# Cache copies issued earlier on the scalar engine, and the end of the second last expert in another order

## What is computed

```python
q, k, v, u = rms(x) @ w_in                       # 12 heads of 64, and 1280 pool channels
x = x + concat(dilated_attention(q, k, v), pool(u) @ pool_w * scale) @ w_out
mk, mv = rms(mem) @ w_ck, rms(mem) @ w_cv        # 256 memory rows of the prompt
x = x + cross_attention(rms(x) @ w_cq, mk, mv) @ w_co
e, gate = route(rms(x))                          # the best 2 experts of one group of 8, 4 groups
x = x + sum(gate * (silu(h @ w_gate[e]) * (h @ w_up[e])) @ w_down[e])
win_k_sample = concat(cache_win_k[:, 1:], k_new) # 8 sequences x 2048 rows x 768 numbers, values alike
```

## Time and profile before

| | us |
|---|---|
| runs shown | 1520.78, 1521.37, 1527.52 |
| median | 1521.37 |
| the profiled execution's own time | 1515.31 |
| its span (first to last instruction) | 1513.5 |
| PE busy | 1271.1 (84%) |
| DVE busy | 531.9 (35%) |
| ACT busy | 167.1 (11%) |
| mean granted clock of PE | 0.885 |

### The profile page before, as it was taken

The page is one execution under the profiler, slowest core; times in us unless marked ns, Lnnn a source line. Parts: engine busy times, 40 slices in busy tenths (PEclk is TensorE's granted clock), DMA queues, the critical chain, the costliest instruction groups (busy, mean ns, idle before and its releaser), DMA issues.

```text
span 1513.5 us, 31182 instructions
## 1 busy us (share of the span) xinstructions
PE 1271.1 (84%) x14012; PEld 741.9 (49%) x14012; DVE 531.9 (35%) x1105; ACT 167.1 (11%) x395; POOL 65.3 (4%) x118
## 2 busy tenths in 40 slices
PE   7999999998999999877778777777777877777776
PEld 4444468765887776443443343334344334333432
DVE  2220155740113326344234334334323433433433
ACT  3100113320111334000000000000000000000000
POOL 2100022221100000000000000000000000000000
PEclk9999999999999999888888788788788878878878
DMA  9999989999999999999999999999999999999997
GB/s 351 347 389 388 352 313 392 381 331 377 389 398 384 367 390 384 385 429 430 435 434 433 430 430 430 435 433 432 432 430 430 433 433 433 433 430 430 433 430 294
DMA packets 87644, 609.43 MB, mean 403 GB/s; under 512 B 6095, under 2 KB 7818, under 8 KB 72722
## 3 DMA queue, kind: packets, MB, share of 16 engines
q1 hardware_dynamic: 44867, 477.13, 75.2%
q10 hardware_dynamic: 34550, 100.80, 18.1%
q0 software_dynamic: 8176, 30.78, 5.8%
HBM read 603.09 MB, written 106.75 MB: 469 GB/s over the span
## 4 chain that ended last, share of the span: by engine, by line
DMA 56%; PE 41%; DVE 2%; issue 1%; ACT 0%; SPq 0%; DVEq 0%; ACTq 0%
DMA ring<-in_w_e_up_dram 46%; PE pb L1152 11%; PE pb L660 7%; PE pb L906 6%; DMA ring<-in_w_in_dram 5%; DMA ring<-in_w_out_dram 5%; PE pb L742 3%; PE pb L1039 2%; PE pb L924 2%; PE pb L686 1%; DMA ring<-in_w_ck_dram 1%; PE pb L710 1%; PE pb L666 1%; PE pb L1186 1%; PE pb L1092 1%
## 5 line engine op out<-in xcount | busy, mean ns | idle before, releaser
L1152 PE MATMUL pb<-ring,xT 128*32 128x128 f32 x8192 | 279.9, 303 | 108.0 <-DMA ring<-in_w_e_up_dram 103.2
L1152 PEld LDWEIGHTS pb<-ring,xT 128*32 128x32 f32 x8192 | 259.0, 123 | 162.8 <-DMA ring<-in_w_e_up_dram 127.4
L2035 DVE TENSOR_TENSOR Z<-pb,Z 128x512 f32<-128x512 f32 x248 | 152.7, 679 | 267.8 <-PE pb L1109 267.8
L1092 PE MATMUL pb<-Z,xT 128*32 128x512 f32 (+1 forms) x768 | 133.9, 789 | 93.5 <-DVE Z L2035 91.5
L1109 PE MATMUL pb<-xT 32*128 32x512 f32 x744 | 172.7, 756 | 0.7 <-DVE Z L2035 0.7
L1186 PE MATMUL pb<-ring,xT 128*32 128x512 f32 x960 | 153.7, 798 | 3.4 <-issue 3.4
L660 PE MATMUL pb<-ring,hreg 128*128 128x512 f32 (+1 forms) x320 | 125.7, 552 | 2.4 <-DMA ring<-in_w_in_dram 2.4
L1092 PEld LDWEIGHTS pb<-Z,xT 128*32 128x32 f32 (+1 forms) x768 | 16.4, 115 | 181.5 <-DVE Z L2035 118.8
L660 PEld LDWEIGHTS pb<-ring,hreg 128*128 128x128 f32 x320 | 60.1, 190 | 64.9 <-issue 59.2
L906 PE MATMUL pb<-hreg,ring 128*128 128x264 f32 x320 | 77.7, 400 | 5.4 <-DMA ring<-in_w_out_dram 5.4
L1186 PEld LDWEIGHTS pb<-ring,xT 128*32 128x32 f32 x960 | 34.8, 141 | 95.6 <-issue 94.9
(11 more groups left out here) (338 smaller groups left out, 1099.3 us busy)
## 6 DMA issues: line engine op xcount, KB each, us to landing
ring<-in_w_e_gate_dram SPq DMA_DIRECT2D x31, 4096.0 KB, 23.2
ring<-in_w_e_down_dram SPq DMA_DIRECT2D x30, 4096.0 KB, 17.6
ring<-in_w_e_up_dram SPq DMA_DIRECT2D x30, 4096.0 KB, 23.7
out_win_k_sample_dram<-in_cache_win_k_dram ACTq DMA_DIRECT2D x24, 1536.0 KB, 15.7
out_win_v_sample_dram<-in_cache_win_v_dram ACTq DMA_DIRECT2D x24, 1536.0 KB, 16.9
ring<-in_w_in_dram SPq DMA_DIRECT2D x7, 4096.0 KB, 33.5
ring<-in_w_out_dram SPq DMA_DIRECT2D x4, 4096.0 KB, 34.7
out_win_k_sample_dram<-in_cache_win_k_dram ACTq DMA_DIRECT2D x8, 1488.0 KB, 15.8
```

The lines of the kernel that those rows point to most:

```text
L1092: last = mm(pb[0][32 * c:32 * c + 32, :], pick[0:n, t, :], xn[0:n, t, 512 * c:512 * c + 512], start=(t == 0), stop=(t == 2))
L1152: last = mm(pb[1][32 * c:32 * c + 32, P * half:P * half + P], XT[:, k, :], w[:, k, P * c:P * c + P], start=(k == 0), stop=(k == KT - 1))
L2035: last = V.tensor_tensor(d, banks[c][:, :], d, ALU.add)
```

## The change

Two edits.

1. The copies that ACT issued in the loop over the pool map (behind tiles 6 and 9) are gone there, and its loop over the turned token tiles issues six instead of four. The count runs on, so the same quarters go out in the same order, and between the two places every call issues a quarter that comes two later.
2. In the second last expert PE runs the sample tokens' `combine` ahead of `gather`, into a bank of its own (`pb[2]`, which else holds the turned gates), `gather` doesn't wait for DVE there, and the gates are turned behind `down`. DVE reads that bank, and its loop ends one expert earlier, with the second last written out.

```diff
                 for t in range(3):
-                    if t == 1 and not (isinstance(i, int) and i < 2):
+                    if t == 1 and not (isinstance(i, int) and (i < 2 or i == NE - 1)):
                         pe.wait_ge(y_added, 3 * i - 4)
...
+                if last_but_one:
+                    combine(i, 2, pb[2:3])
+                    gather(i + 1)
+                    return
                 if not last_of_all:
                     gather(i + 1)
...
+            def down_and_gates():
+
+                pe.wait_ge(hidT_ready, NE - 1)
+                down(NE - 2)
+                pe.wait_ge(y_added, 3 * (NE - 2))
+                turn_gates(NE - 2)
+
             with pe.If(n_over > 0):
-                down(NE - 2)
+                down_and_gates()
...
             with pe.Else():
-                down(NE - 2)
+                down_and_gates()
...
             for k in range(KT):
                 freed(copy(xT[:, k, :], filled("x")[:, 0:TOK]))
-                if k % 4 == 3:
+                if k in (1, 3, 5, 7, 11, 15):
                     cache_part()
...
                 freed(nc.scalar.mul(mixP[:, j, :], filled("map")[:, 0:TOK], gT[:, 4 * KT + j:4 * KT + j + 1]))
-                if j in (6, 9):
-                    cache_part()
...
-                    add_results(i, 2, pb[0:1] if last_of_all else pb[4:8])
+                    last_but_one = isinstance(i, int) and i == NE - 2
+                    add_results(i, 2, pb[0:1] if last_of_all else pb[2:3] if last_but_one else pb[4:8])
...
-            with dve.Fori(1, NE - 1) as i:
+            with dve.Fori(1, NE - 2) as i:
                 expert(i)
+            expert(NE - 2)
```

## The result

The changed kernel takes 1524.47 us, median of 20 runs (1519.33 to 1537.9); the kernel before, in the same session on the same chip, 1520.57, median of 20. The ratio is 1.0037, 95% interval 1.0020 to 1.0054: 5.6 us slower (3.0 to 8.2). The ratio and its interval come from all the runs; the two medians alone lie 3.9 us apart. The time lies within the range and within the 0.5% that the prediction called no change, but on the other side: it had forecast 2.4 us faster.

What follows compares the result with a forecast made beforehand. The prediction took weight transfers to set the pace from 643 us on, with PE busy nearly throughout before 590. Its terms, 3.6 - 4.2 - 1.8 = -2.4 us, gave 1519.0 us against a median of 1521.37; range 1512 to 1529.

Steps and rivals of the forecast that it cites:

- the hold: Loop over the token tiles: ACT's copy issues held at 55.6 until about 62, briefly at 61.3, and again at 67.0.
- the 12: Sign against the forecast: ACT held over 12 us in the loop over the token tiles would mean a slower kernel.
- The front: Token tiles to w_in: the extra copy issues delay PE's start on w_in by 3.6 us, bounds 0 and 10.
- the gap at 192 us: Transfers stand still from 192 to 199 us, share 0.27; this was to swallow the two extra copies in ACT's queue.
- The middle: Pool map to output projection: without the copies the first w_out piece lands sooner and PE gains 4.2 us.
- the 2.83 and 1.75 us of waiting: PE's waits for the first w_out piece and for the last sequence's value rows, counted as available gain.
- the middle gives nothing: Rival: other traffic fills the room in the pool map, or later w_out pieces are waited for; 1523.2 us, chance 0.15.
- The end: Last two experts: work comes 3.0 us sooner, limited by the last down weights to a gain of 1.8 us.
- the wait for the last quarter: Last product: PE waits for the last quarter of the down weights, which leaves only 1.6 us of room.
- the 3.44 us ... stay: Second last expert: the 3.44 us stop at the count read and branch ahead of `down` remains.
- the long hold: Rival: ACT held at tiles 11 and 15, tiles 12 to 15 and DVE's scaling 10 us late; 1525.4 us, chance 0.2.
- The rule of the Trainium skill: Copy issues at the front: starting transfers usually takes little time, so the front is near nothing, sum -6.0 or a little less.

Runs made afterwards that it cites:

- the second ones: Changed kernel and kernel before, each profiled and timed once more without an edit: ratios to the kernel before 1.0056 and 0.9993.
- behind the squares: Kernel before with the two pool-map copies issued right after the squares of the memory keys, four among the token tiles as before: 1520.54 us, ratio 0.9997.
- put nowhere: Kernel before without the two pool-map copies, so 3 MB of the last sequence's values are never copied: 1518.98 us, ratio 0.9987.
- into the hole: Kernel before with the two pool-map copies issued at about 191 us, behind the second square of the tokens' heads: 1518.52 us, ratio 1.0017.
- the last version: Kernel before plus edit 2, five token-loop copies, one left in the pool map, and two copies of 198 to 199 us issued at 191: 1515.60 us, ratio 0.9963.

## Why the prediction was wrong

**The step that failed is the hold, "for a moment at 61.3".** Its rule was four copies in the queue, the small part counted as one, and the fifth held. By it the issue behind tile 7 was the fifth and held until about 62, which came true (62.25), and the landing of the first copy made room for the next one. But the small part takes no place, as its landing at 66.6 freed nothing: the issue behind tile 11 is again the fourth large copy, and had to wait until the second large one was through, whose landing the prediction itself had put at 73.6 to 76.5 (it was 75.6). It was held for 10.32 us instead of a moment, and with the 6.73 before it ACT stood for over 17 us in the loop, past the 12 that the prediction gave as a sign of being wrong. With that, the last four tiles came late, and DVE's scaling, not the square, set the path: the square at 78.02 still came ahead of the scaling's end at 80.64. The front measured 7.2 us at w_in's start in the first profile, 7.3 between the second ones and 5.9 at w_in's third piece, against 3.6 forecast. And the gap at 192 us swallowed next to nothing: it came some 7 us later, with PE (DMA share 0.38 from 199 to 206 us in the first profile of the changed kernel, 0.29 in the second).

**The middle, -4.2, came out near zero.** Two things. The copy's traffic was priced as 4.3 us, all of it off the piece's landing; the table shows 1.4 to 3.3 in eight profiles of ten, and nothing in two. And the base was wrong: the 2.83 and 1.75 us of waiting were read in an execution in which PE kept its clock through the pool map; in half the profiles, of before too, it doesn't, and then PE comes to w_out late anyway. The three runs that take both copies out of the map and leave w_in's start alone came out 0.5 us faster (behind the squares), 2.0 faster (put nowhere) and 2.6 slower (into the hole): none shows a gain that can be told from zero. The case "the middle gives nothing", at 0.15, was nearly right on this, for another reason than it gave: in half the profiles it is not other traffic, but a slow PE that hides the landing.

**The end, -1.8, was right in size**: 1.8 in the first pair of profiles, 2.1 (4.4 faster to 0.2 slower) alone. From the end of the up product to the end of the span it is 48.4 to 49.2 us in the seven profiles without this edit, and 46.3 to 47.8 in six of the seven with it (50.9 in the last version). Of its parts, the wait for DVE went and the wait for the last quarter came, as forecast. The step "the 3.44 us ... stay" was wrong: the stop at the count read and the branch takes 4.71 to 5.11 us in the seven profiles with this edit, and 2.67 to 4.06 in the seven without. Why it is longer when PE arrives without having waited wasn't tried. That the last expert still began 2.9 us sooner, where 3.0 were forecast, is luck. With the wait of 3.03 some 1.7 us more went, which the prediction hadn't counted: the products behind that wait ran at a granted clock of 0.66 before (1469.94 to 1475.00 us), and at 1.00 without it (1489.24 to 1494.10 after). This paid for the longer stop.

**The sum.** With the measured terms, 6.3 for the hold (5.8 and 0.5, the first edit alone against the same copies behind the squares), -0.5 for the rest of that edit and -2.1 for the end, it is +3.7, inside the 3.0 to 8.2 of the first timing and below the 5.9 to 10.9 of the second; each of the three terms is itself known only to some 2 to 5 us. The rival that ended on the other side, the long hold, gave 1525.4 where 1524.47 was measured; its mechanism was the right one (tiles 12 to 15 late, DVE's scaling with them), but its number owes something to luck, since its 10 us at the front were 6 to 7 and its -4.2 in the middle about nothing.

**The rule of the Trainium skill** that the prediction set against its front, that starting a transfer usually takes little time against the transfer itself ("DMA: Bandwidth & Descriptors", section "Issuing engines are not separate DMA queues"), would have the front near nothing. Issues of 6.73 and 10.32 us, for copies that landed 29.8 and 28.7 us after their issue began, decide against it here, on a queue that already holds three copies of 1.5 MB.

## What to carry to other kernels

Count what an engine's DMA queue already holds, in large transfers, at every place where that engine issues one more: behind an issue that is held, all that the engine does next is late, so put issues in excess behind work that nobody waits for. Before a wait is priced as gain, look in a second profile whether it is there: a wait that only exists when TensorE kept its clock is worth nothing in the other executions. And room in the transfers is best filled with copies that else ride beside a load that is waited for: here that load then took 26.8 to 32.1 us instead of 33.5 to 39.5. What it gives to the whole wasn't resolved.

## What the runs showed of the hardware that was not expected

The fourth large copy on ACT's queue (1.5 MB, memory to memory) stops the engine until the oldest of three is nearly through: 10.32 us at 62.38, where the queue, sharing with two others, moved 1.36 MB in those 10.3 us. A small part of 45 KB takes no place, but is held like the others when the places are taken (4.45 us at 72.83). And one and the same stretch of products, behind the same wait of about 2 us, ran at the full clock in some executions and at half in others of the same program (4.74 and 8.66 us). In the two profiles of the kernel before, that moved PE's start on the output projection from 38.9 to 43.2 us behind the issue of its first weights, nearly as much as the 5.6 us of the whole change.
